# One core, three fused transformer blocks: branch products of the third block from rounded parts, and held chunks in its two last token projections

## The chip, the cores and the metric

The kernel runs on one core of one Trainium2 chip, in one launch. The metric is the device time of that core in microseconds. Two engines matter most here: PE (TensorE) does the matrix products, ACT (ScalarE) and DVE (VectorE) prepare operands and take results out of PSUM. POOL and SP mostly issue DMAs.

## The reference

Three blocks follow each other on x, 512 tokens by 1024 features, in fp32. The change touches only the end of the third one. `h` and `h2` are modulated norms of x; `ret`, `four`, `sgu` are the retention, Fourier and gated branches.

```
z = h @ w_in                                   # ..., gates (3 x 1024)
ga, gb, gc = split(sigmoid(gates), 3)
merged = ga*(ret @ w_a) + gb*(four @ w_b) + gc*(sgu @ w_c)   # ret: 512 wide, four and sgu: 256 wide
y = merged @ w_o
x = x + gt1 * rms_norm(y, g_post_mix)
h2 = rms_norm(x, g_pre_mlp) * (1 + sc2) + sh2
a = relu(h2 @ w_up)
x = x + gt2 * rms_norm((a*a) @ w_down, g_post_mlp)
```

## The kernel before

**Layout.** Features lie on the 128 partitions, so a tensor of 1024 features is 8 tiles of 128x512 (features by tokens). Weights come in chunks of 512 KB (128x1024 floats) through a ring of four SBUF slots, `weight_ring` (`c.slot`), by DMAs that SP issues in the order of the list STAGES. A stage of kind "loop" or "branch" is a hardware loop on every engine.

**Split products.** Most stages compute an fp32 product from rounded parts: ACT copies a weight chunk into `weight_hi` (type fp32r, `round_chunk`), DVE writes the rest `weight - hi` into `weight_lo` (`rest_chunk`), and PE adds three products: hi with hi, hi with lo, lo with hi, each a 128x512 matmul. `weight_hi` and `weight_lo` hold two chunks (SPLIT_RING = 2), so chunk n+2 can be rounded only when the products with chunk n are done. Activations have such parts too: `H_hi`/`H_lo`, `mid_hi`/`mid_lo`. The semaphore `w_rounded` counts ACT's rounds, `w_split` DVE's rests; SP refills a slot when its chunk is split. Stages that are not split use the fp32 operands directly; PE's trace then shows two MATMUL records for each product.

**Banks.** Two rings of four PSUM banks each: `proj_banks` for the projections, `mix_banks` for everything else. PE waits for a bank's `empty` semaphore and raises `full`.

**The stages at the change**, in the order in which PE works:

- The Fourier product ("four", L1470 and L1471) and the 32 small products of the gated branch ("sgu", L1478) end the mixing. DVE turns the two sgu banks into `cond` tiles (L2285); ACT copies the four banks out.
- "br", the branch stage (L1480 to L1507 on PE, `gate_tiles` on ACT, `branch_tiles` on DVE): eight output tiles, each from four chunks. Three chunks hold the gates' weights and make three split products of 24 matmuls (L1498). The fourth holds the columns of w_a, w_b and w_c for this tile; it is not split: PE multiplies it directly with `T(8..11)` and four `late_tile`s (L1505), 4 + 2 + 2 fp32 products into three banks. PE waits for the mixed branches (`mixed`, `four`, `sgu_ready`) ahead of the whole loop. ACT takes the gates out with a sigmoid, DVE multiplies and adds, and splits the merged tile into two parts (`merged_hi`, `merged_lo`).
- "ro", the output projection, a token stage (`token_stage`, L1509 to L1546): output tiles are 128 tokens by 512 features, two halves (`part`) of four token tiles each, every half contracted over four chunks. The chunk is the outer loop, the four token tiles the inner one, except that the last two chunks of the second half are contracted by token tile: all of token tile 0 first, then tile 1, and so on, so that tiles end one after another. These two chunks (6 and 7) are "held": their parts go to a place of their own (`c.held`) instead of the ring of two. `root_token`, `root_residual` on ACT and `gained`, `new_residual`, `token_scales` on DVE turn each token tile into the new x and its norm's scale.
- The hand-over to "upr" (the MLP's up projection) goes by halves of 256 tokens: `half_turned` (L1554) turns x back to features by tokens and scales it, into four banks "ht"; ACT (`round_half`) writes the rounded part, DVE (`split_half`) recomputes the unrounded value from the same bank and subtracts; `half_pair` multiplies the first two tiles of upr, first with the rounded part (L1568), then with the rest (L1572). Then follows the loop `split_loop` (L875).
- "dnr", the down projection, is a token stage over 16 chunks a half, with its last two chunks contracted by token tile as well, but none held: chunk 31 takes the place of chunk 29 in the ring of two.

Each engine executes its instructions strictly in the order of its program; the order across engines is set by the semaphores alone. `st.done` and `st.last` make an engine also wait for its own instruction.

Of the kernel before, what the change touches and what calls it, by code (L numbers as in the profile page):

```python
# [324 lines left out]
class Chip:  # L325


    def __init__(self, nc, ctx, dram):
# [37 lines left out]
        with ExitStack() as mlstm:  # L366
# [26 lines left out]
            "pr_ready", "sgu_ready", "merged", "relu_ready", "mlp_raw", "mlp_hi", "mlp_mid", "grow_diag", "y_sq", "y_root", "x_new", "h10_root", "h10_diag", "h10_hi", "h10_raw", "h10_lo", "out_ready", "out_stored",  # L393
# [136 lines left out]
    def held(self, n):  # L530

        return tuple(self.relu_r[:, at * S:(at + 2) * S] for at in (4 * n, 4 * n + 2))
# [124 lines left out]
def sync_program(nc, sp, c):  # L657
# [14 lines left out]
    for stage in STAGES:  # L672
# [20 lines left out]
        if looped:  # L693
            per = len(pieces(kt))
            use0 = proj.number[(name, 0)]
            with sp.Fori(1, total // RING) as i:
                for q in range(RING):
                    if kind == "branch":
                        if q < 3:
                            sp.wait_ge(s["w_split"], 3 * (i - 1) + (c.first_split[name] + q + 1))  # L700
                        else:
                            sp.wait_ge(proj.full_sem, 6 * (i - 1) + (use0 + 6))
                    elif name in SPLIT:
# [13 lines left out]
def chunk_use(c, chunk):  # L717

    name = [s[0] for s in STAGES if c.first_chunk[s[0]] <= chunk][-1]
    if name in SPLIT and (name != "br" or (chunk - c.first_chunk[name]) % 4 < 3):  # L720
        n = chunk - c.first_chunk[name]
        return c.sem["w_split"], c.first_split[name] + (n if name != "br" else 3 * (n // 4) + n % 4) + 1
# [5 lines left out]
    elif kind == "branch":  # L728
        t = 6 * (n // 4) + (n % 4 if n % 4 < 3 else 5)
# [71 lines left out]
def tensor_program(nc, pe, c):  # L801
# [681 lines left out]
    use0, chunk0 = proj.number[("br", 0)], c.first_chunk["br"]  # L1483
    pe.wait_ge(s["mixed"], MIXED_M + 4)
    pe.wait_ge(*mix.emptied(("four", 1)))
    pe.wait_ge(s["sgu_ready"], 2)
    with pe.Fori(0, 4) as i:
        for j in range(12):
            u, n, g = use0 + j, j // 6, j % 6
            pe.wait_ge(proj.empty_sem[u % RING], i * 3 + u // RING)  # L1490
            ch = chunk0 + 4 * n + min(g, 3)
            if g < 3:
                sn = c.first_split["br"] + 3 * n + g
                pe.wait_ge(s["w_split"], i * 6 + (sn + 1))
                for k in range(KD):
                    w = slice(k * P, (k + 1) * P)
                    for m, (stationary, moving) in enumerate(((c.hi, hi9), (c.hi, c.H_lo), (c.lo, hi9))):
                        last = mm(proj.banks[:, u % RING, :], stationary(sn)[:, w], moving(k), start=k + m == 0, stop=k == KD - 1 and m == 2)  # L1498
                last.then_inc(proj.full_sem, 1)
                continue  # L1500
            pe.wait_ge(c.landed[ch % RING], i * 32 + 16 * (ch // RING + 1))
            srcs = [[T(8 + k) for k in range(4)], [c.late_tile(2), c.late_tile(3)], [c.late_tile(4), c.late_tile(5)]][g - 3]
            at = (0, 4, 6)[g - 3]
            for k, src in enumerate(srcs):
# [4 lines left out]
    def token_stage(name, hi, lo, held, ready=None):  # L1509
# [3 lines left out]
        def products(n, part, q, t, whole=None):  # L1513
# [3 lines left out]
            w_hi, w_lo = whole or (c.hi(first + n), c.lo(first + n))  # L1517
# [8 lines left out]
        for part in range(2):  # L1526
            for q in range(chunks if part == 0 else chunks - 2):
# [9 lines left out]
        for t in range(NB):  # L1537
            for q in range(chunks - 2, chunks):
# [1810 lines left out]
```

## Time and profile before

| what | value |
|---|---|
| median of 3 runs | 3490.22 us (3490.09 to 3494.72) |
| the profiled execution | 3490.96 us, its span 3489.3 us |
| PE busy, share of the span | 3370.3 us, 97% |
| DVE, ACT busy | 1995.6 us (57%), 1098.5 us (31%) |
| HBM traffic | 357.66 MB read, 103 GB/s over the span |

The span runs from the first to the last recorded instruction; 1.66 us of the execution lie around it. PE's matmuls are pipelined: the record of a 128x512 matmul of rounded parts lasts 389 ns, but the next one starts sooner. Intervals from start to start tell what a matmul costs, not the records' lengths. PEclk is the granted clock of TensorE, 1.00 for the upper of its two levels (2.4 GHz) and 0.50 for the lower (1.2 GHz).

### The profile page before, as it was taken

What the parts mean: (1) busy time and instruction counts of PE and PEld (TensorE: products, weight loads), DVE (VectorE), ACT (ScalarE), POOL (GpSimd) and SP (SyncE); (2) the same over time, 40 slices, a digit from 0 to 9 for tenths busy, and PEclk for the clock granted to TensorE, in tenths of its full rate; (3) what the DMA queues carried; (4) which work ended last, traced back from release to release, by engine and by line L of the source; (5) the groups of instructions that cost most, each with busy time, mean ns of one, the idle gap of its engine ahead of it and who ended that gap; (6) DMA issues with size and microseconds to landing.
All of it is one profiled execution on the core that took longest, in us unless ns stands there. A gap on an engine that the chain in (4) does not pass through costs nothing. (4 is left out here: it accounts for less than half of the span.)

```text
span 3489.3 us, 38628 instructions
## 1 busy us (share of the span) xinstructions
PE 3370.3 (97%) x13776; PEld 2507.8 (72%) x13776; DVE 1995.6 (57%) x2807; ACT 1098.5 (31%) x1491; POOL 134.1 (4%) x230
## 2 busy tenths in 40 slices
PE   6999999999899999999999999999999999999999
PEld 3446778887678887667788854678887656778887
DVE  6685666535668864465665369666634543355522
ACT  2223422224532222453333200443333341142222
POOL 1000000000000000000000040000000100000000
PEclk9999999999999999999999999999999999999999
DMA  7222355542125542212223311122333222222232
GB/s 285 79 67 85 117 187 192 172 133 66 49 97 192 192 143 86 79 43 85 85 97 96 95 55 49 54 90 96 94 99 127 67 73 79 90 85 86 94 101 81
DMA packets 100426, 361.20 MB, mean 104 GB/s; under 512 B 11152, under 2 KB 11168, under 8 KB 100064
## 3 DMA queue, kind: packets, MB, share of 16 engines
q1 hardware_dynamic: 79088, 280.34, 24.1%
q0 software_dynamic: 20080, 75.27, 6.4%
q10 hardware_dynamic: 1152, 4.19, 0.3%
q8 instruction: 65, 1.06, 0.1%
q14 instruction: 41, 0.34, 0.0%
HBM read 357.66 MB, written 2.10 MB: 103 GB/s over the span
## 5 line engine op out<-in xcount | busy, mean ns | idle before, releaser
L2285 DVE TENSOR_TENSOR weight_lo<-weight_ring,weight_hi 128x1024 fp32r<-128x1024 f32 (+1 forms) x458 | 552.9, 1208 | 941.0 <-ACT weight_hi L1599 935.4
L1599 ACT ACTIVATE weight_hi<-weight_ring 128x1024 fp32r<-128x1024 f32 (+1 forms) x458 | 478.5, 1045 | 1641.2 <-PE proj_banks L875 1001.8
L875 PE MATMUL proj_banks<-h_lo,weight_hi 128*128 128x512 f32 x1704 | 664.9, 390 | 0.0
L875 PE MATMUL proj_banks<-h_hi,weight_hi 128*128 128x512 f32 x1344 | 523.9, 390 | 4.0 <-DVE weight_lo L2285 4.0
L875 PE MATMUL proj_banks<-h_hi,weight_lo 128*128 128x512 f32 x1344 | 523.5, 389 | 0.0
L875 PEld LDWEIGHTS proj_banks<-h_lo,weight_hi 128*128 128x128 f32 x1704 | 321.0, 188 | 66.6
L875 PEld LDWEIGHTS proj_banks<-h_hi,weight_hi 128*128 128x128 f32 x1344 | 252.6, 188 | 57.9 <-issue 5.7
L875 PEld LDWEIGHTS proj_banks<-h_hi,weight_lo 128*128 128x128 f32 x1344 | 252.7, 188 | 52.7
L875 PE MATMUL proj_banks<-mid_hi,weight_hi 128*128 128x512 f32 x704 | 273.9, 389 | 0.0
L875 PE MATMUL proj_banks<-mid_lo,weight_hi 128*128 128x512 f32 x704 | 273.9, 389 | 0.0
L875 PE MATMUL proj_banks<-mid_hi,weight_lo 128*128 128x512 f32 x704 | 273.9, 389 | 0.0
L821 PE MATMUL proj_banks<-h_tiles,weight_ring 128*128 128x512 f32 x528 | 233.3, 599 | 3.5 <-ACT h_tiles L1599 3.5
L821 PEld LDWEIGHTS proj_banks<-h_tiles,weight_ring 128*128 128x128 f32 x528 | 101.8, 193 | 131.7 <-issue 129.9
L2293 DVE SCALAR_TENSOR_TENSOR scratch<-proj_banks,vectors,scratch 128x511 f32<-128x511 f32 (+3 forms) x208 | 155.2, 746 | 26.3 <-ACT scratch L1599 12.7
L2285 DVE TENSOR_TENSOR scratch<-scratch 128x512 f32<-128x512 f32 (+6 forms) x218 | 154.3, 708 | 12.2 <-ACT scratch L1599 2.5
L875 PEld LDWEIGHTS proj_banks<-mid_lo,weight_hi 128*128 128x128 f32 x704 | 132.2, 188 | 27.5
L875 PEld LDWEIGHTS proj_banks<-mid_hi,weight_hi 128*128 128x128 f32 x704 | 132.2, 188 | 27.4
L875 PEld LDWEIGHTS proj_banks<-mid_hi,weight_lo 128*128 128x128 f32 x704 | 132.2, 188 | 27.4
L2293 DVE SCALAR_TENSOR_TENSOR scratch<-scratch,vectors 128x512 f32<-128x512 f32 x190 | 142.9, 752 | 6.7
L1599 ACT ACTIVATE scratch<-proj_banks 128x512 f32<-128x512 f32 (+1 forms) x178 | 100.7, 572 | 117.5 <-PE proj_banks L821 68.2
L1599 ACT ACTIVATE scratch<-proj_banks,vectors 128x512 f32<-128x512 f32 x112 | 83.9, 749 | 159.9 <-PE proj_banks L821 159.9
L1599 ACT ACT_TABLE_LOAD x70 | 89.8, 1283 | 54.6 <-PE proj_banks L821 13.3
(402 smaller groups left out, 5132.3 us busy)
## 6 DMA issues: line engine op xcount, KB each, us to landing
weight_ring<-in_w_up SPq DMA_DIRECT2D x176, 512.0 KB, 3.3
ada_ring<-in_ada POOLq DMA_DIRECT2D x96, 512.0 KB, 3.8
weight_ring<-in_w_dn SPq DMA_DIRECT2D x64, 512.0 KB, 3.5
weight_ring<-in_w_br SPq DMA_DIRECT2D x32, 512.0 KB, 3.2
weight_ring<-in_w_upr SPq DMA_DIRECT2D x32, 512.0 KB, 3.2
weight_ring<-in_w_dnr SPq DMA_DIRECT2D x32, 512.0 KB, 3.2
weight_ring<-in_w_dn SPq DMA_DIRECT2D x32, 384.0 KB, 3.1
cond<-in_ada POOLq DMA_DIRECT2D x20, 512.0 KB, 4.6
```

Source lines behind the costliest of these rows:

```text
L821: last = mm(bank[:, 0:n], c.slot(chunk)[:, i * P:(i + 1) * P], rhs(k), start=k == 0, stop=k == sum(per) - 1)
L875: last = mm(proj.banks[:, u % RING, :], stationary(split0 + n)[:, w], moving(k), start=k + m == 0, stop=k == kt - 1 and m == 2)
L1599: return nc.scalar.activation(out, in_, func, **kw)
L2285: return v.tensor_tensor(out, a, b, op)
L2293: return v.scalar_tensor_tensor(out=out, in0=a, scalar=x, in1=b, op0=op0, op1=op1)
```

## The change

- The fourth chunk of each branch tile is split too (`splits_of`: 32 rounds instead of 24), and the branch products become three products of rounded parts. The eight branch operands get rounded parts: ACT's `branch_round` writes them to `H_hi`, DVE writes the rests to free tiles. PE's three waits ahead of the loop go; it waits for `branch_lo`, k by k, inside the branch products.
- ro: chunks 5, 6 and 7 are held, and these three are contracted by token tile.
- The residual's square sum is one ACT instruction over 1024 values instead of two over 512 with an addition of eps between them.
- The hand-over: PE turns half 1 ahead of the products with half 0's rests; the unrounded values of two of the four ht banks (1 and 3) are made by ACT (`raw_half`) instead of DVE; the order of the rests is 0, 1, 4, 5, 2, 3, 6, 7; several self-waits go; the scales of token tiles 2 and 3 are made inside DVE's `split_half(0)`.
- dnr: chunk 31 is held in `h_rounded`; the squares that used this place as scratch go elsewhere.

```diff
 def splits_of(stage):
-    return 24 if stage[0] == "br" else chunks_of(stage)
+    return chunks_of(stage)
...
+    def branch_hi(self, k):
+        return self.H_hi(k)
+
+    def branch_lo(self, k):
+        if k < 4:
+            return self.mid_hi[:, (8 + k) * S:(9 + k) * S]
+        return self.late_r[:, (k - 2 if k < 6 else k) * S:(k - 1 if k < 6 else k + 1) * S]
+
+    def held(self, name, n):
+        if name == "ro" and n >= 5:
+            return tuple(self.relu_r[:, at * S:(at + 2) * S] for at in (4 * (n - 5), 4 * (n - 5) + 2))
+        if name == "dnr" and n == F3T - 1:
+            return tuple(self.h_r[:, at * S:(at + 2) * S] for at in (4, 6))
+        return None
...
# PE, branch stage
-    pe.wait_ge(s["mixed"], MIXED_M + 4)
-    pe.wait_ge(*mix.emptied(("four", 1)))
-    pe.wait_ge(s["sgu_ready"], 2)
     with pe.Fori(0, 4) as i:
         for j in range(12):
             u, n, g = use0 + j, j // 6, j % 6
             pe.wait_ge(proj.empty_sem[u % RING], i * 3 + u // RING)
-            ch = chunk0 + 4 * n + min(g, 3)
-            if g < 3:
-                sn = c.first_split["br"] + 3 * n + g
...
-            pe.wait_ge(c.landed[ch % RING], i * 32 + 16 * (ch // RING + 1))
...
-                last = mm(proj.banks[:, u % RING, :], c.slot(ch)[:, (at + k) * P:(at + k + 1) * P], src,
-                          start=k == 0, stop=k == len(srcs) - 1)
+            sn = c.first_split["br"] + 4 * n + min(g, 3)
+            pe.wait_ge(s["w_split"], i * 8 + (sn + 1))
+            at, count = ((0, KD), (0, KD), (0, KD), (0, 4), (4, 2), (6, 2))[g]
+            hi, lo = (hi9, c.H_lo) if g < 3 else (c.branch_hi, c.branch_lo)
+            for k in range(at, at + count):
+                if g >= 3:
+                    pe.wait_ge(s["branch_lo"], k + 1)
+                w = slice(k * P, (k + 1) * P)
+                for m, (stationary, moving) in enumerate(((c.hi, hi), (c.hi, lo), (c.lo, hi))):
+                    last = mm(proj.banks[:, u % RING, :], stationary(sn)[:, w], moving(k), start=k == at and m == 0,
+                              stop=k == at + count - 1 and m == 2)
             last.then_inc(proj.full_sem, 1)
...
# PE, token stages
-            for q in range(chunks - 2, chunks):
-                last = products(chunks + q, 1, q, t, held and held(q - chunks + 2))
+            for q in range(chunks - together, chunks):
+                last = products(chunks + q, 1, q, t)
...
-    for half in range(2):
-        half_turned(half)
-        half_pair(half)
+    half_turned(0)
+    half_pair(0)
+    half_turned(1)
+    half_rest(0)
+    half_pair(1)
+    half_rest(1)
...
+REST_ORDER = (0, 1, 4, 5, 2, 3, 6, 7)
...
# ACT
+    for h in range(4):
+        branch_round(h, T(8 + h))
     for t in range(2):
+        act.wait_ge(*mix.filled(("four", t)))
+        branch_round(4 + t, mix.bank(("four", t)))
         copy_out(mix, ("four", t), c.late_tile(2 + t))
+    for t in range(2):
+        act.wait_ge(s["sgu_ready"], t + 1)
+        branch_round(6 + t, c.late_tile(4 + t))
...
-            for g in range(3):
-                u = u0 + 6 * n + g
+            for g in range(4):
+                u = u0 + 6 * n + (g if g < 3 else 5)
                 act.wait_ge(proj.full_sem, i * 12 + u + 1)
-                ahead = 3 * n + g + SPLIT_RING
+                ahead = 4 * n + g + SPLIT_RING
...
     def root_residual(t):
-        for p in range(2):
-            act.wait_ge(s["x_new"], 2 * t + p + 1)
-            st.link(f(T(32).rearrange("p (k f) -> p k f", k=4), c.x_token(t, p), ACT.Square, accum_out=c.x_stat(p, t)))
-            if p == 0:
-                st.link(f(c.x_bias(t), c.x_stat(0, t), ACT.Identity, scale=1.0 / D, bias=eps))
-        st.done(f(c.x_scale(t), c.x_stat(1, t), ACT.Sqrt, scale=1.0 / D, bias=c.x_bias(t)), s["h10_root"])
+        act.wait_ge(s["x_new"], 2 * t + 2)
+        x = c.x[:, :].rearrange("p (k j f) -> p k j f", k=KD, j=NB)[:, :, t, :]
+        st.link(f(c.T(55, 2).rearrange("p (k f) -> p k f", k=KD), x, ACT.Square, accum_out=c.x_stat(0, t)))
+        st.done(f(c.x_scale(t), c.x_stat(0, t), ACT.Sqrt, scale=1.0 / D, bias=eps), s["h10_root"])
...
+    def raw_half(half):
+        use, layer, part, _ = MODULATED[10]
+        for b in (1, 3):
+            for k in range(2 * b, 2 * b + 2):
+                if half == 1:
+                    act.wait_ge(s["h10_lo"], KD)
+                bank = mix.bank(("ht", half, b))[:, k % 2 * 256:(k % 2 + 1) * 256]
+                ins = f(c.raw_half(k), bank, ACT.Identity, scale=c.g(use, k), bias=c.m(layer, part, k))
...
-    round_chunk("ro", 5)
-    for n in range(2):
-        round_to("ro", 6 + n, c.held(n)[0])
+    for n in range(5, KD):
+        round_to("ro", n, c.held("ro", n)[0])
...
     round_half(0)
-    for t in range(2, 4):
-        root_residual(t)
+    root_residual(2)
+    root_residual(3)
+    raw_half(0)
     for n in range(SPLIT_RING):
         round_chunk("upr", SPLIT_RING + n)
     round_half(1)
+    raw_half(1)
...
-    for n in range(17, F3T):
+    for n in range(17, F3T - 1):
         round_chunk("dnr", n)
+    round_to("dnr", F3T - 1, c.held("dnr", F3T - 1)[0])
...
# DVE
+    for k in range(KD):
+        dve.wait_ge(s["branch_hi"], k + 1)
+        if k in (4, 5):
+            dve.wait_ge(*mix.emptied(("four", k - 4)))
+        tt(c.branch_lo(k), c.branch_raw(k), c.branch_hi(k).bitcast(F32), ALU.subtract).then_inc(s["branch_lo"], 1)
...
             for g in range(3):
...
+                rest_br(i, 4 * n + g + SPLIT_RING, last)
             for g in range(3):
                 u = u0 + 6 * n + 3 + g
...
+            rest_br(i, 4 * n + 3 + SPLIT_RING, last)
...
     def split_half(half):
-        for b in range(4):
-            dve.wait_ge(s["h10_hi"], KD * half + 2 * b + 2)
+        for b in (0, 2, 1, 3):
+            bank = mix.bank(("ht", half, b))
+            if half == 0 and b == 1:
+                for t in range(2, 4):
+                    token_scales(t)
+            if b % 2 == 0:
+                dve.wait_ge(s["h10_hi"], KD * half + 2 * b + 2)
...
+            else:
+                dve.wait_ge(*mix.emptied(("ht", half, b)))
```

## Rows read from the trace of the kernel before

**Rows 1.** The page: busy time of each engine, share of the span, instructions.

```profile
PE 3370.3 (97%) x13776; PEld 2507.8 (72%) x13776; DVE 1995.6 (57%) x2807; ACT 1098.5 (31%) x1491; POOL 134.1 (4%) x230
```

**Rows 2.** Waits of PE from 2870 us on: us in total, times, longest.

```profile
PE proj_banks L1498 <- DVE cond L2285: 4.0, 1, 4.0
PE proj_banks L1572 <- DVE h_lo L2285: 2.7, 3, 1.2
PE proj_banks L1523 <- DVE weight_lo L2285: 2.4, 1, 2.4
PE mix_banks L1554 <- DVE scratch L2289: 2.2, 2, 1.7
```

**Rows 3.** Stretches: us, busy time of PE, PEld, DVE, ACT, POOL, granted clock, DMA, GB/s.

```profile
2882.40:2887.60 5.20, 5.18 (x12) 4.14 (x13) 0.00 (x0) 0.00 (x0) 0.00 (x0) 0.51 0.00 0
2887.60:3070.10 182.50, 182.50 (x693) 130.01 (x692) 63.15 (x76) 38.53 (x50) 0.00 (x0) 1.00 0.24 84
...
3140.00:3143.50 3.50, 3.50 (x11) 2.76 (x10) 2.51 (x5) 1.08 (x2) 0.00 (x0) 0.51 0.00 0
3471.00:3474.40 3.40, 3.40 (x10) 2.67 (x9) 0.00 (x0) 0.00 (x0) 0.00 (x0) 0.52 0.00 0
```

**Rows 4.** Timeline, mixing to branch stage: start us, us, instruction [idle before].

```profile
2876.42 1.97 PE L1478 MATMUL mix_banks<-cond,scratch 128*64 128x128 f32 x32
...
2876.59 0.60 ACT L1599 ACTIVATE ada_ring<-mix_banks 128x512 f32<-128x512 f32 x1 [1.10 <-PE mix_banks L1471]
...
2877.20 1.28 ACT L1599 ACT_TABLE_LOAD   x1
...
2881.28 0.69 DVE L2285 TENSOR_TENSOR cond<-cond,scratch 128x512 f32<-128x512 f32 x1
...
2882.42 0.79 PE L1498 MATMUL proj_banks<-mid_hi,weight_hi 128*128 128x512 f32 x1 [4.03 <-DVE cond L2285]
```

**Rows 5.** The chain that ended last, one branch tile: start us, us, what.

```profile
2908.27 16.33 PE proj_banks L1498 x72
2924.61 6.87 PE proj_banks L1505 x16
```

**Rows 6.** Timeline, branch stage: a round, its rest, an evacuation.

```profile
2901.52 1.06 ACT L1599 ACTIVATE weight_hi<-weight_ring 128x1024 fp32r<-128x1024 f32 x1 [3.97 <-PE proj_banks L1498]
...
2902.61 1.22 DVE L2285 TENSOR_TENSOR weight_lo<-weight_ring,weight_hi 128x1024 fp32r<-128x1024 f32 x1 [4.29 <-ACT weight_hi L1599]
...
2908.31 0.69 DVE L2285 TENSOR_TENSOR scratch<-proj_banks,scratch 128x512 f32<-128x512 f32 x1 [0.30 <-PE proj_banks L1505]
```

**Rows 7.** Timeline, output projection, second half: statistics, then rests of held chunks.

```profile
3093.26 0.30 ACT L1599 ACTIVATE small<-small,others 128x4 f32<-128x4 f32 x1
...
3095.90 2.35 DVE L2285 TENSOR_TENSOR relu_hi<-weight_ring,relu_hi 128x1024 fp32r<-128x1024 f32 x2
```

**Rows 8.** Timeline, token tile 0 after its last product.

```profile
3106.08 0.60 ACT L1599 ACTIVATE scratch<-proj_banks 128x512 f32<-128x512 f32 x1 [5.70 <-PE proj_banks L1523]
...
3107.72 1.54 DVE L2293 SCALAR_TENSOR_TENSOR x_tiles<-scratch,small,x_tiles 128x512 f32<-128x512 f32 x2
```

**Rows 9.** Timeline, hand-over to the up projection.

```profile
3115.90 3.84 PE L1554 MATMUL mix_banks<-scratch,x_tiles 128*128 128x128 f32 x32 [1.70 <-DVE scratch L2289]
...
3117.18 4.75 ACT L1599 ACTIVATE late_rounded<-mix_banks,mod,gain 128x256 fp32r<-128x256 f32 x8 [0.88 <-PE mix_banks L1554]
...
3118.58 1.12 DVE L2290 TENSOR_SCALAR scratch<-mix_banks,gain,mod 128x256 f32<-128x256 f32 x2
...
3119.50 4.08 PE L1568 MATMUL proj_banks<-late_rounded,relu_lo 128*128 128x256 f32 x32
...
3135.95 2.02 PE L1572 MATMUL proj_banks<-h_lo,relu_lo 128*128 128x256 f32 x12
...
3140.01 0.57 PE L875 MATMUL proj_banks<-late_rounded,weight_hi 128*128 128x512 f32 x1
```

**Rows 10.** Timeline, down projection: first product of its two last chunks.

```profile
3470.62 0.50 PE L1523 MATMUL proj_banks<-weight_hi,h_rounded 128*128 128x512 f32 x1 [2.41 <-DVE weight_lo L2285]
```

More of the change, by code:

```diff
@@ L528, in ro_out, with branch_raw, raw_half @@
         return self.T(24 + 4 * p + t)
-    def held(self, n):
-        return tuple(self.relu_r[:, at * S:(at + 2) * S] for at in (4 * n, 4 * n + 2))
+    def branch_raw(self, k):
+        return self.T(8 + k) if k < 4 else self.late_tile(k - 2)
+    def branch_hi(self, k):
[10 more added lines that the diff above has]
+        return None
+    def raw_half(self, k):
+        return self.pool[:, 12 * S + k * 256:12 * S + (k + 1) * 256]
     def first_up(self, t):
@@ L697, in sync_program @@
                 for q in range(RING):
[L698 to L703, printed above, removed]
+                    if name in SPLIT:
                         sp.wait_ge(s["w_split"], RING * (i - 1) + (c.first_split[name] + q + 1))
@@ L719, in chunk_use @@
     name = [s[0] for s in STAGES if c.first_chunk[s[0]] <= chunk][-1]
[L720 to L722 removed]
+    if name in SPLIT:
+        return c.sem["w_split"], c.first_split[name] + chunk - c.first_chunk[name] + 1
     _, kind, tiles, kt = STAGE[name]
@@ L1507, in tensor_program, with token_stage, products @@
             last.then_inc(proj.full_sem, 1)
-    def token_stage(name, hi, lo, held, ready=None):
+    def token_stage(name, hi, lo, together, ready=None):
         chunks, first = STAGE[name][3] // 2, c.first_split[name]
-        def products(n, part, q, t, whole=None):
+        def products(n, part, q, t):
             key = (name, NB * part + t)
             bank = open_bank(proj, key) if q == 0 else proj.bank(key)
-            w_hi, w_lo = whole or (c.hi(first + n), c.lo(first + n))
+            w_hi, w_lo = c.held(name, n) or (c.hi(first + n), c.lo(first + n))
@@ L1526, in token_stage @@
         for part in range(2):
-            for q in range(chunks if part == 0 else chunks - 2):
+            for q in range(chunks if part == 0 else chunks - together):
                 n = chunks * part + q
@@ L3082, in vector_program, with rest_br @@
         st.done(tt(c.late_tile(4 + t), c.late_tile(4 + t), T(35 + t), ALU.mult), s["sgu_ready"])
-    u0 = proj.number[("br", 0)]
+    for k in range(KD):
[3 more added lines that the diff above has]
+        tt(c.branch_lo(k), c.branch_raw(k), c.branch_hi(k).bitcast(F32), ALU.subtract).then_inc(s["branch_lo"], 1)
+    u0 = proj.number[("br", 0)]
+    def rest_br(i, ahead, last):
+        if last and ahead >= 8:
+            rest_chunk("ro", ahead - 8)
+            return
+        split, chunk = c.first_split["br"] + ahead, c.first_chunk["br"] + ahead
+        dve.wait_ge(s["w_rounded"], i * 8 + (split + 1))
+        tt(c.lo(split), c.slot(chunk), c.hi(split).bitcast(F32), ALU.subtract).then_inc(s["w_split"], 1)
     def branch_tiles(i, last=False):
@@ L3089, in branch_tiles @@
             for g in range(3):
-                ahead = 3 * n + g + SPLIT_RING
-                if last and ahead >= 6:
-                    rest_chunk("ro", ahead - 6)
-                else:
-                    split, chunk = c.first_split["br"] + ahead, c.first_chunk["br"] + 4 * (ahead // 3) + ahead % 3
-                    dve.wait_ge(s["w_rounded"], i * 6 + (split + 1))
-                    tt(c.lo(split), c.slot(chunk), c.hi(split).bitcast(F32), ALU.subtract).then_inc(s["w_split"], 1)
+                rest_br(i, 4 * n + g + SPLIT_RING, last)
             for g in range(3):
@@ L3163, in vector_program @@
         gained("ro", 0, t, c.ro_out(t, 0), c.gain_row(0, 0), 0)
-    rest_chunk("ro", 5)
-    for n in range(2):
-        rest_to("ro", 6 + n, c.held(n))
+    for n in range(5, KD):
+        rest_to("ro", n, c.held("ro", n))
     for n in range(2):
@@ L3175, in vector_program @@
     split_half(0)
-    for t in range(2, 4):
-        token_scales(t)
     for n in range(SPLIT_RING):
@@ L3216, in vector_program @@
         gained("dnr", 0, t, c.late_tile(t), c.gain_row(1, 0), 8)
-    for n in range(17, F3T):
+    for n in range(17, F3T - 1):
         rest_chunk("dnr", n)
+    rest_to("dnr", F3T - 1, c.held("dnr", F3T - 1))
     for t in range(NB):
```

87 lines of the change are left out of this document (42 added, 45 removed).

## Prediction, made before the changed kernel had been run

> **What bounds the kernel now.** The page first: PE is busy for 97% of the span, DVE for 57%, ACT for 31% [rows 1]. So the time is PE's, and an edit can bring only three things: less work for PE, fewer waits of PE, or less time at the lower clock. The waits of PE in the last 620 us are few: 4.0 us ahead of the branch stage, 2.2 and 2.7 us in the hand-over to upr, 2.4 us near the end of dnr [rows 2]. The stretches show the clock: it is 1.00 in 2887.6 to 3070.1, but 0.51 to 0.52 in three short stretches that begin at or just behind such a wait, 5.2, 3.5 and 3.4 us long [rows 3]. The chain gives the price of a branch tile: 72 products of the gates in 16.33 us, which is 0.2268 us each, then 8 direct fp32 products (16 records) in 6.87 us, 0.859 us each [rows 5].
>
> **The start of the branch stage.** PE's last small products end at 2876.42 + 1.97 = 2878.4; it then waits for DVE's second `cond` tile, ready at 2881.97, and starts at 2882.42 [rows 4]. The gates need none of it, and after the change nothing holds them: 4.0 us less. The 5.2 us at 0.51 behind it [rows 3] cost 5.2 x 0.49 = 2.5 us, of which I leave 0.4 for a first product that is slow in any case (0.79 us [rows 4]). Together 6.1 us. If the small products, not the wait, bring the clock down, only 4.0.
>
> What is added lies beside the gates. ACT: six rounds and two copies while the mixing ends, the last two rounds behind DVE's `cond` tiles, 0.60 us each [rows 4]: done at about 2882.7; then its table load and a tiny instruction, 1.5 us: 2884.2. Gate 0's products end at 2878.4 + 5.44 = 2883.8, so the round of chunk 2 (1.06 us [rows 6]) ends at 2885.3. DVE: eight rests at about 0.72 us with the gap (0.69 [rows 4]) from 2882.0 on, to 2887.8, and behind them in its queue the rest of chunk 2 (1.22 us [rows 6]), 2889.0. PE wants chunk 2 after two gates, at 2889.3. It fits, by 0.3 us; I take 0 and keep up to 1 us for it. The new waits for `branch_lo` come at 2894.7: long satisfied.
>
> **The branch products.** Eight fp32 products (6.87 us) become 24 of rounded parts: 24 x 0.2268 = 5.44 us. 1.43 us x 8 tiles = **11.4 us** [rows 5]. This stands if the rounding keeps up. Each tile adds one round and one rest, so ACT has 4 x 1.06 + 3 x 0.58 = 6.0 us of work and DVE 4 x 1.22 + 6.3 = 11.2 us (three multiplications and two additions at 0.69, the merged tile's split at about 1.1, gaps) in 21.8 us. Before they had 38.5 and 63.2 us in 182.5 [rows 3]. The order holds too: the branch chunk is rounded when gate 1 is done and split 2.6 us later, 2.8 us before product a wants it; the next tile's second chunk is rounded when product c is done, split behind two evacuations some 2.7 us later, and wanted 5.44 us later. Queued behind it on DVE are the two instructions for the merged tile, which ro wants only chunks later. SP refills a slot at the split instead of after the products: earlier, never later; the bytes stay the same. Cost of all this: 0, its cover the 21.8 us of PE. The waits inside the products, 64 in all, I price at 0: the gates' loop has two satisfied waits for each 24 products and still runs at 0.2268 us a product [rows 5]. The upper bound is the first product after a change of operands, recorded with 0.79 us where an ordinary one has 0.39, so 0.4 us each [rows 4].
>
> **ro with three held chunks.** PE was done with ro at 3115.90 - 1.70 = 3114.2 [rows 9]. Four token tiles of 12 products (10.9 us) and two whole chunks (10.9 us) lie ahead of that, so the second half began at 3092.4. Now chunk 4 is done at 3097.85, and all rests must be there: ACT's statistics end at 3093.56 [rows 7], three rounds follow, and DVE's third rest ends at 3095.90 + 2.35 = 3098.25 [rows 7]; these instructions and their order stay, only their targets change. PE waits 0.5 us. Then four token tiles of 18 products, 4.08 us each, from 3098.4 to 3114.7: 0.5 us later than before. In exchange the tiles end further apart. From a tile's end to its new x are 3.2 us (3106.08 to 3107.72 + 1.54 [rows 8]). Tile 2 ends at 3110.6, its x is there at 3113.9, and behind it in DVE's queue the scales of tile 1 at 3114.4, for ACT has only one square of about 1.06 us to do (as a round of 1024 values [rows 6]) and a root. So half 0 is turned at 3114.8 rather than 3115.90: **1.1 us**. The wait of 1.7 us is gone, half a us of it comes back as the wait for rests.
>
> **The hand-over.** Before: 3115.90 to 3140.01, 24.1 us [rows 9]. Now: the turn takes 3.6 us (3115.90 to 3119.50), to 3118.4; the 32 products with rounded parts 3.9, to 3122.3. The next turn needs the scales of tile 3. Its x is there at 3118.0; ACT is busy with the rounds of half 0 until about 3120.4 (eight took 4.75 us [rows 9]), then two squares with their roots, 1.5 us each, to 3123.4, then DVE's 0.5: 3123.9. So PE's next wait is here, 1.5 us. Turn to 3127.5; half 0's 16 rests, 2.0 us, which have been ready since about 3127 (12 took 2.02 at worst [rows 9]), to 3129.5; rounded parts of half 1 to 3133.4, for ACT's `raw_half(0)` and two weight rounds (4 us) leave its rounds of half 1 at 3127.5 to 3132; the rests, whose last needs ACT's raw values at 3134 and DVE's 0.9, to 3135.4. That is 20.6 us, **3.5 us** less: DVE's 1.12 us for a pair of raw values [rows 9] no longer stand four times in each half's path.
>
> The clock fell to 0.51 at 3140.0 [rows 3] after a series of short waits; 3.5 x 0.49 = 1.7 us. Waits of 0.5, 1.5 and some 0.3 us remain, so I leave this fall in. The Trainium skill (TensorE: Matmul & The Clock Gate, section on psum-queue depth-cycling) says that frequent micro-idles between groups of matmuls let the clock swing between its levels. By this rule too the fall stays, and my sum is unchanged; without it the sum would be 1.7 us better. The trace agrees, with no wait over 1.7 us in this stretch and a clock of 0.51 behind it.
>
> **dnr.** The wait of 2.4 us at 3470.62 is for chunk 31's round and rest, which follow chunk 29 [rows 2, 10]. Held, chunk 31 follows chunk 30's round at once, a chunk earlier. The wait goes, and the fall behind it, 3.4 x 0.48 = 1.6 us [rows 3]: **4.0 us**. The tail behind PE stays.
>
> **Sum.** 6.1 + 11.4 + 1.1 + 3.5 + 4.0 = 26.1 us off the profiled execution's 3490.96 us: 3464.9. The median lies 0.7 us lower: **3464.1 us**. With the lower bounds (3.0, 11.0, 0.4, 1.5, 2.6) it is 18.5 us, 3471.7; with the upper ones (6.4, 11.6, 1.6, 6.0, 4.4) 30 us, 3460.2.
>
> **Rivals.**
> - *The clock takes back.* It falls at the branch stage all the same (2.1 us) and a second time in the hand-over (1.7 us, as at 3140). For it: the products at 2876.42 use half the array's columns, and all waits in the hand-over stay short. Against: those rows show one fall in the hand-over, not two. Median 3490.2 - 22.3 = 3467.9.
> - *The hand-over gains more.* ACT without self-waits is quicker than 0.59 us a round, the third wait shrinks and the clock holds: 3.5 + 1.7 + 1 more, 3461.
> - *The new waits cost.* 64 x 0.4 = 25.6 us: nothing is left, 3489.7. Against: the gates' rate.
> - *Slower: the branch chunk comes late.* Place: PE's wait for `w_split` ahead of product a. If it is over 4.8 us late against my schedule (2.8 us of slack, then 2 us), PE waits 2 us in each tile, and each wait brings a fall of some 2.5 us as at 2882.4: 8 x 4.5 = 36 us, 3500. It decides from a loss of 3.3 us a tile, and costs over 0.2% from 4.1. Against: both preparing engines are over 40% idle in this stage.
> - *The change does not do what it says* at dnr or at the first wait: another semaphore of the same moment, a DMA's, holds PE. Then 4 to 6 us of the gain are missing, 3469.
>
> **Chances.** Forecast 0.70, clock 0.12, more gain 0.07, missing wait 0.06, waits that cost 0.03, slower 0.02. Differences under about 0.2% (7 us) a measurement of this kernel can't tell from none. Hence faster 0.95, same 0.03, slower 0.02. The range takes in both clock cases and most of the missing wait: 3459.5 to 3471.
>
> **What would show it.** Right: no wait ahead of L1498 and a granted clock of 1.00 from its start; a branch tile in 21.8 us instead of 23.2; the turn of half 0 at the end of ro with no wait, a wait of 1 to 2 us ahead of the turn of half 1; no PE wait in dnr. Wrong: a wait for `weight_lo` inside the branch stage, products there over 0.23 us apart, or a hand-over over 23 us.

## The result, and the profile after

| | before | after |
|---|---|---|
| median | 3490.68 us (4 runs, 3490.09 to 3494.72) | 3464.94 us (4 runs, 3461.79 to 3468.48) |
| profiled execution | 3490.96 us, span 3489.3 | 3468.48 us, span 3466.8 |

The ratio is 0.9924, with a 95% interval of 0.9907 to 0.9941. The forecast was 3464.1 us, in a range of 3459.5 to 3471.

The page of the kernel after, to be read beside [rows 1]:

```profile
PE 3355.3 (97%) x13840; PEld 2517.3 (73%) x13840; DVE 2003.4 (58%) x2815; ACT 1110.9 (32%) x1503; POOL 134.1 (4%) x230
```

PE has 64 records more (192 for the branch products instead of 128) and is busy for 15 us less: three products of rounded parts take less than a direct one, and behind 2880 us less time passes at the lower clock (ahead of it more, see `after_again`).

PE's waits from 2850 us on, in the columns of [rows 2]:

```profile
PE mix_banks L1560 <- DVE scratch L2331: 0.9, 1, 0.9
PE proj_banks L1529 <- DVE relu_hi L2327: 0.4, 1, 0.4
PE mix_banks L1479 <- ACT ada_ring L1613: 0.4, 1, 0.4
```

The waits of 4.0 us ahead of the branch stage and of 2.4 us in the down projection are gone, and those of the hand-over have shrunk from 4.9 to 0.9 us. One of 0.4 us is new, on a rest of the three held chunks. (The last row is ahead of the change, where the kernel before has the same wait.)

How the late stages lie, in the columns of [rows 3]: branch stage, output projection, hand-over, up projection, down projection.

```profile
2884.90:3059.10 174.20, 174.20 (x770) 144.29 (x769) 79.45 (x97) 47.25 (x59) 0.00 (x0) 1.00 0.28 94
3059.10:3103.30 44.20, 43.77 (x193) 35.78 (x191) 24.14 (x34) 19.59 (x35) 0.00 (x0) 1.00 0.32 107
3103.30:3123.20 19.90, 19.00 (x161) 18.75 (x161) 15.24 (x34) 17.14 (x35) 0.00 (x0) 1.00 0.17 54
3123.20:3286.40 163.20, 163.20 (x722) 135.19 (x722) 85.69 (x116) 45.88 (x60) 0.00 (x0) 1.00 0.28 93
3286.40:3460.40 174.00, 174.00 (x770) 144.07 (x768) 51.41 (x55) 39.26 (x50) 0.00 (x0) 1.00 0.26 88
```

The granted clock is 1.00 in all five. The kernel before had 0.51 to 0.52 in three stretches of this part [rows 3].

From stage start to stage start, read off the first product of each stage in both traces:

| stretch | before | after | gain | forecast |
|---|---|---|---|---|
| first gated product to the first gate product | 6.0 | 1.9 | 4.1 | 4.0 |
| branch stage | 187.7 | 174.2 | 13.5 | 2.1 + 11.4 |
| output projection to the first turn | 45.8 | 44.3 | 1.5 | 1.1 |
| hand-over | 24.1 | 19.9 | 4.2 | 3.5 |
| up projection | 164.8 | 163.2 | 1.6 | 0 |
| down projection to the start of its last product | 178.2 | 173.9 | 4.3 | 4.0 |
| tail | 6.3 | 6.5 | -0.2 | 0 |
| sum, from unrounded values | 612.9 | 583.8 | 29.1 | 26.1 |

But the first gated product, the last piece ahead of the change, starts at 2882.99 us here and at 2876.42 before [rows 4], 6.6 us later, in code that both kernels share. So the profiled execution gained 22.5 us, the changed part 29.1. The run `after_again` deals with this.

The start of the branch stage, PE's timeline of the kernel after:

```profile
2882.99 1.97 PE L1492 MATMUL mix_banks<-cond,scratch 128*64 128x128 f32 x32
2884.89 0.50 PE L1511 MATMUL proj_banks<-mid_hi,weight_hi 128*128 128x512 f32 x1
```

The gates follow the small products with no idle time, at full rate. The first gate product takes 0.50 us where the one before took 0.79 [rows 4].

The chain of the kernel after, whose rows merge what [rows 5] shows apart:

```profile
2884.96 174.30 PE proj_banks L1511 x768
3059.27 21.77 PE proj_banks L1529 x96
```

The eight branch tiles are 768 products in 174.3 us without a break: 0.227 us each, 21.79 us a tile. The output projection's first half follows at the same rate.

### The profile page after: what moved, and what is told of

It reads as the page before. It is cut to its first block and busy times, and to the rows that moved or that the text cites. A ratio compares the mean times of both kernels' runs of the same rounds, so it can differ in the third digit from the quotient of the medians.

```text
span 3466.8 us, 38774 instructions
## 1 busy us (share of the span) xinstructions
PE 3355.3 (97%) x13840; PEld 2517.3 (73%) x13840; DVE 2003.4 (58%) x2815; ACT 1110.9 (32%) x1503; POOL 134.1 (4%) x230
## 3 DMA queue, kind: packets, MB, share of 16 engines
q8 instruction: 65, 1.06, 0.1%
## 5 line engine op out<-in xcount | busy, mean ns | idle before, releaser
L2327 DVE TENSOR_TENSOR weight_lo<-weight_ring,weight_hi 128x1024 fp32r<-128x1024 f32 (+1 forms) x464 | 560.2, 1208 | 914.3 <-ACT weight_hi L1613 908.0
```

The lines of the kernel that those rows point to most:

```text
L2327: return v.tensor_tensor(out, a, b, op)
```

## The experiments

All stretches below are measured in the profiled execution of each run, from the start of a stage's first product, since the time ahead of 2876 us differs between executions by more than most of the effects. The medians, beside 3490.58 us of the kernel before, are 3468.82 for `dnr_ring`, 3470.32 for `handover_back` and 3462.44 for `ro_two`; the stretches tell what these can't. `order_back`, `raw_back`, `more_waits`, `rests_late2` and `rests_late3` ran once each.

### The wait alone

`start_alone` is the kernel before with one edit.

```diff
-    pe.wait_ge(s["mixed"], MIXED_M + 4)
-    pe.wait_ge(*mix.emptied(("four", 1)))
-    pe.wait_ge(s["sgu_ready"], 2)
     with pe.Fori(0, 4) as i:
...
+            if j == 3:
+                pe.wait_ge(s["mixed"], MIXED_M + 4)
+                pe.wait_ge(*mix.emptied(("four", 1)))
+                pe.wait_ge(s["sgu_ready"], 2)
             pe.wait_ge(c.landed[ch % RING], i * 32 + 16 * (ch // RING + 1))
```

> The kernel before, with one edit: PE's three waits for the mixed branches stand ahead of the first direct branch product instead of ahead of the whole branch loop. Theory (the wait and the fall of the clock behind it are separate from the products' price): PE starts the gates 4.0 us earlier, the granted clock stays 1.00, the stretch from the first gated product (2876.4 us before) to the end of the span shrinks from 612.9 us by 6.1 us to about 606.8, a branch tile still takes 23.2 us. Rival (the small products with half the array's columns bring the clock down): only 4.0 us less, a stretch at 0.51 behind the start. Rival (the direct products take the wait over): 0 us.

Median 3483.76 us against 3490.58, ratio 0.9977 (0.9967 to 0.9988). In its trace the gates begin 1.9 us behind the first gated product, and the branch stage takes 185.3 us. Three stretches: branch stage, one inside the hand-over, up projection.

```profile
2878.30:3063.60 185.30, 185.30 (x706) 132.33 (x705) 66.64 (x82) 38.90 (x52) 0.00 (x0) 1.00 0.23 82
...
3122.90:3126.30 3.40, 3.40 (x18) 3.40 (x18) 3.06 (x6) 2.25 (x4) 0.00 (x0) 0.50 0.52 167
3133.60:3296.80 163.20, 163.20 (x723) 135.11 (x721) 85.69 (x116) 45.90 (x60) 0.00 (x0) 1.00 0.27 93
```

The clock is 1.00 in the branch stage. The gain there is 4.1 + (187.7 - 185.3) = 6.5 us, near the expected 6.1, and the small products do not bring the clock down. With the same upper clock and no wait, 185.3 against 174.2 us is the price of the products alone: **11.1 us**, with the 2.4 us of the fall apart. The whole part behind the first gated product took 603.2 us, 9.7 less than before. The other 3.2 us came from two falls of the clock: the one that stood behind the hand-over now lies inside it (second row), where it costs nothing: the hand-over still takes 24.2 us, since PE waits there for ACT and DVE anyway. And the down projection lost none:

```profile
PE proj_banks L1524 <- DVE weight_lo L2286: 2.4, 1, 2.4
```

The whole down projection of this run, in the columns of [rows 3]:

```profile
3296.80:3473.20 176.40, 174.00 (x768) 143.77 (x767) 51.39 (x55) 39.37 (x50) 0.00 (x0) 1.00 0.25 87
```

The same wait of 2.4 us as in [rows 2], but no stretch at the lower clock behind it.

### The held last chunk

`dnr_ring` is the kernel after, with chunk 31 back in the ring of two.

```diff
-    for n in range(17, F3T - 1):
+    for n in range(17, F3T):
         round_chunk("dnr", n)
-    round_to("dnr", F3T - 1, c.held("dnr", F3T - 1)[0])
```

> The changed kernel, with chunk 31 of the down projection back in the ring of two. Theory: PE waits 2.4 us for its rest again and the clock falls to half for some 3.4 us behind it; from the first product of the up projection's loop to the end 4.0 us more than in the changed kernel. Rival (the held chunk is only a by-product, the wait is a DMA's): 0 us. Rival (the clock would have stayed up): 2.4 us.

Its waits of PE in the down projection, and the stretch behind the wait:

```profile
PE proj_banks L1527 <- DVE weight_lo L2324: 2.4, 1, 2.4
```

```profile
3447.10:3450.50 3.40, 3.40 (x10) 2.63 (x9) 0.00 (x0) 0.66 (x2) 0.00 (x0) 0.50 0.00 0
```

The down projection takes 178.2 us against 173.9, 4.3 us more. In `start_alone`, with the same wait and no fall, it took 176.6, so 2.7 of them are the wait with the restart behind it and 1.6 the lower clock. The rival by which a DMA holds PE falls. The term of 4.0 us stands when a fall follows the wait, as here and in the kernel before; where none follows, the held chunk would be worth 2.7.

### The hand-over, whole and by its edits

`handover_back` is the kernel after with the hand-over's functions of before (three held chunks stay). `order_back` and `raw_back` undo one edit each.

```diff
# order_back
     half_pair(0)
-    half_turned(1)
     half_rest(0)
+    half_turned(1)
# raw_back
     root_residual(3)
-    raw_half(0)
...
     round_half(1)
-    raw_half(1)
...
-            if b % 2 == 0:
+            if True:
                 dve.wait_ge(s["h10_hi"], KD * half + 2 * b + 2)
```

> The changed kernel, with the hand-over to the up projection as before: halves one after the other, all unrounded values by DVE, two squares for a residual, self-waits back. Three held chunks stay. Theory: from the first turn to the up projection's loop 24.1 us instead of 20.0, with waits of DVE's rests and of scales, and the clock falls to 0.51 behind it: 4.1 + 1.7 = 5.8 us more in all. Rival (the fall at 3140 us before was an accident of its moment): 4.1 us. Rival (the gain comes from the earlier ends of token tiles 0 to 2, not from the hand-over's own edits): under 1 us.

> The changed kernel, with one edit of the hand-over undone: PE multiplies half 0's rests ahead of the turn of half 1. Theory: the rests of banks 1 and 3 come behind the scales in DVE's queue, so PE waits for them some 3 us after the first products, then turns half 1 and waits for the first rounded tile: 2 to 4 us more in the hand-over (19.9 us). Rival: the order is worth nothing, since the same products wait for the same rests: 0 to 0.5 us more.

> The changed kernel, with one edit of the hand-over undone: DVE makes all unrounded values, ACT none. Theory: DVE does 4 x 0.5 us more in each half, ACT 2.1 us less; in half 0 the rests still end while PE turns half 1 (0 to 1 us), in half 1 ACT's rounds start 2 us earlier but DVE's last rest ends about 1 us later: 0 to 1.5 us more in the hand-over (19.9 us). Rival: this split is what the hand-over's gain comes from: 3 to 4 us more.

`handover_back`, PE's waits for rests in the hand-over, and the stretch at the lower clock inside it:

```profile
PE proj_banks L1578 <- DVE h_lo L2305: 3.6, 3, 1.2
```

```profile
3109.00:3112.40 3.40, 2.91 (x13) 2.62 (x14) 3.10 (x5) 0.30 (x1) 0.00 (x0) 0.50 0.08 11
```

The hand-over takes 26.0 us, 6.1 more than after, near the expected 5.8 in size. But the fall lay inside the hand-over and not behind it (the up projection takes 163.2 us, its full rate). The old hand-over took 24.1 and 24.2 us in the kernel before and in `start_alone`, without a fall that cost anything. Where the other 1.9 us lie shows in PE's two turns, first of `handover_back`, then the second one of the kernel before:

```profile
3096.47 3.84 PE L1560 MATMUL mix_banks<-scratch,x_tiles 128*128 128x128 f32 x32
...
3109.99 4.98 PE L1560 MATMUL mix_banks<-scratch,x_tiles 128*128 128x128 f32 x32 [0.49 <-DVE scratch L2309]
```

```profile
3128.44 3.84 PE L1554 MATMUL mix_banks<-scratch,x_tiles 128*128 128x128 f32 x32 [0.54 <-DVE scratch L2289]
```

From the first turn to the second are 13.5 us against 12.5 before (3115.90 to 3128.44, [rows 9]), and from there to the up projection 12.5 against 11.6. The second difference, 0.9 us, is the clock: the fall lies on the turn, 4.98 us instead of 3.84. The first, 1.0 us, is not. PE turns half 0 earlier, but DVE, still at token tile 3, starts half 0's unrounded values 3.5 us behind the turn (at 3100.01), where before it started 2.7 us behind it [rows 9]; that is 0.9 of the 1.0 us. So without the fall the old hand-over would take 25.1 us behind three held chunks, and its edits are worth 5.2 us there: without them, 1.0 us of what the output projection gained is lost again. The rival by which the earlier token tiles bring the gain falls.

The two single edits, PE's waits of `order_back` and of `raw_back`:

```profile
PE proj_banks L1582 <- DVE h_lo L2327: 0.9, 1, 0.9
```

```profile
PE mix_banks L1560 <- DVE scratch L2329: 0.9, 1, 0.9
PE proj_banks L1582 <- DVE h_lo L2325: 0.9, 1, 0.9
```

`order_back`: 20.6 us, 0.6 more. Half 0's rests wait 0.9 us for DVE, but this wait stands where the other one stood: with the rests first, the scales for the second turn are ready in time. So the order is worth 0.6, nearer to its rival than to my 2 to 4. I had both waits in my account, though PE can serve one while the other runs out. `raw_back`: 21.5 us, 1.6 more, with a second wait of 0.9 us at half 1's last rests, a little above the expected 0 to 1.5. What is left, 5.2 - 0.6 - 1.6 = 3.0 us, belongs to the single square, the self-waits, the place of the scales and what the edits do only together; these were not tried apart.

The kernel after, PE and then ACT in the hand-over, beside [rows 9]:

```profile
3103.35 3.84 PE L1560 MATMUL mix_banks<-scratch,x_tiles 128*128 128x128 f32 x32
3106.95 4.08 PE L1574 MATMUL proj_banks<-late_rounded,relu_lo 128*128 128x256 f32 x32
3111.92 3.84 PE L1560 MATMUL mix_banks<-scratch,x_tiles 128*128 128x128 f32 x32 [0.90 <-DVE scratch L2331]
3115.52 2.16 PE L1582 MATMUL proj_banks<-h_lo,relu_lo 128*128 128x256 f32 x16
3117.52 4.00 PE L1574 MATMUL proj_banks<-late_rounded,relu_lo 128*128 128x256 f32 x32
3121.36 2.08 PE L1582 MATMUL proj_banks<-h_lo,relu_lo 128*128 128x256 f32 x16
```

```profile
3104.65 3.76 ACT L1613 ACTIVATE late_rounded<-mix_banks,mod,gain 128x256 fp32r<-128x256 f32 x8
...
3109.80 1.06 ACT L1613 ACTIVATE scratch<-x_tiles 128x1024 f32<-128x1024 f32 x1
...
3111.32 2.07 ACT L1613 ACTIVATE scratch<-mix_banks,mod,gain 128x256 f32<-128x256 f32 x4
```

Eight rounds take 3.76 us without the self-waits instead of 4.75, a residual's square 1.06. PE's only wait stands ahead of the second turn, 0.9 us where I had 1.5.

### Two held chunks or three

`ro_two` is the kernel after with the output projection as before: chunk 5 in the ring, two chunks by token tile.

```diff
-        if name == "ro" and n >= 5:
+        if name == "ro" and n >= 6:
...
-    token_stage("ro", ..., 3, lambda k: (s["merged_lo"], k + 1))
+    token_stage("ro", ..., 2, lambda k: (s["merged_lo"], k + 1))
```

> The changed kernel, with two held chunks in the output projection, contracted by token tile, as before; chunk 5 goes through the ring of two. Theory: the wait of 0.4 us for rests goes, but the scales of token tile 1 come after PE's last product, and PE waits 1.0 to 1.7 us ahead of the first turn: 0.5 to 1.3 us more from the start of the output projection to the up projection's loop. Rival (three held chunks bring nothing, for ACT's single square alone makes the scales early enough): 0.4 us less.

```profile
3095.00 3.84 PE L1560 MATMUL mix_banks<-scratch,x_tiles 128*128 128x128 f32 x32 [1.51 <-DVE scratch L2332]
```

From the output projection's start to the first turn 45.2 us against 44.3: **0.9 us** for the third held chunk. The wait of 1.5 us is back, nearly the old 1.7 [rows 9], and the one for rests is gone. So of the 1.5 us that this stage gained, 0.9 came with the third chunk, and 0.6 with the rest of the change: 0.4 of it at the stage's first product, which lasts 0.79 us behind the direct products of the kernel before and 0.39 here, and 0.2 in the shorter wait.

### Do waits on PE cost?

`more_waits` puts a satisfied wait ahead of each of the 768 products.

```diff
                 for m, (stationary, moving) in enumerate(((c.hi, hi), (c.hi, lo), (c.lo, hi))):
+                    pe.wait_ge(s["mixed"], MIXED_M)
                     last = mm(...)
```

> The changed kernel, with a wait on a long satisfied semaphore ahead of every product of the branch stage, 768 more waits. Theory (a satisfied wait on PE is hidden by the product that runs): a branch tile takes 21.8 us as before, the stage 174.2 us. Rival (each wait costs what I feared in the prediction's third rival, up to 0.4 us): 768 x 0.4 = 307 us more; at 0.02 us each 15 us more.

```profile
2876.20 174.30 PE proj_banks L1512 x768
```

174.30 us for the stage, to the hundredth what it took without them. A satisfied wait on PE costs nothing behind a running product of 0.227 us; this rival had a chance of 0.03 and deserved less.

### Where slower would begin

`rests_late2` and `rests_late3` let DVE do two or three reductions that nobody needs ahead of each rest in the branch stage; no result changes.

```diff
         dve.wait_ge(s["w_rounded"], i * 8 + (split + 1))
+        for extra in range(3):
+            at = 8 + 3 * (ahead - SPLIT_RING) + extra
+            v.tensor_reduce(small[:, at:at + 1], c.slot(chunk), AX.X, ALU.add)
         tt(c.lo(split), c.slot(chunk), c.hi(split).bitcast(F32), ALU.subtract).then_inc(s["w_split"], 1)
```

> The changed kernel, with two extra reductions of 1.22 us each on DVE ahead of every rest in the branch stage: every rest is 2.4 us late. Theory (slack of 2.8 us for three of four chunks, 2.1 us for the one behind the evacuations): the stage takes 174.2 us plus 8 x 0.3 us plus up to 1.5 us at its start, 177 to 178 us. Rival (DVE has no slack worth the name in this stage): 8 x 4 x 2.4 = 78 us more.

> The changed kernel, with three extra reductions on DVE ahead of every rest in the branch stage: every rest is 3.7 us late. Theory (the slower rival of the prediction begins where the slack of 2.1 to 2.8 us ends): each tile loses 3 x 0.8 + 1.5 = 3.9 us, the stage takes about 205 to 208 us, and with waits of 0.8 to 1.5 us the clock falls at times. Rival (the ring of two evens it out over a tile, since DVE has 21.8 us for 26 us of work at most): under 10 us more.

`rests_late2`: 186.3 us, 12.1 more than 174.2; I expected 3 to 4. DVE's timeline shows the cause (the last row is PE's):

```profile
2943.63 2.35 DVE L3142 TENSOR_REDUCE small<-weight_ring 128x1 f32<-128x1024 f32 x2 [1.96 <-ACT weight_hi L1613]
...
2945.89 1.22 DVE L2327 TENSOR_TENSOR weight_lo<-weight_ring,weight_hi 128x1024 fp32r<-128x1024 f32 x1
...
2947.90 0.69 DVE L2327 TENSOR_TENSOR scratch<-proj_banks,scratch 128x512 f32<-128x512 f32 x1 [0.19 <-DVE scratch L2327]
...
2951.15 2.35 DVE L3142 TENSOR_REDUCE small<-weight_ring 128x1 f32<-128x1024 f32 x2 [0.23 <-DVE scratch L2327]
...
2953.41 1.22 DVE L2327 TENSOR_TENSOR weight_lo<-weight_ring,weight_hi 128x1024 fp32r<-128x1024 f32 x1
...
2954.69 0.50 PE L1511 MATMUL proj_banks<-mid_hi,weight_hi 128*128 128x512 f32 x1 [1.31 <-DVE weight_lo L2327]
```

The rest for the next tile's first chunk now ends at 2947.1, and the evacuations of products a, b and c queue behind it. Products a and b are already done; against the kernel after, the evacuations end some 1.2 us later in the tile, and only then do the reductions and the rest of the next tile's second chunk begin. It ends at 2954.6, 3.5 us late where I had counted 2.4, and PE has waited 1.3 us. In the kernel after the same two rests run free of each other:

```profile
2902.64 1.23 DVE L2327 TENSOR_TENSOR weight_lo<-weight_ring,weight_hi 128x1024 fp32r<-128x1024 f32 x1 [4.21 <-ACT weight_hi L1613]
...
2908.77 1.23 DVE L2327 TENSOR_TENSOR weight_lo<-weight_ring,weight_hi 128x1024 fp32r<-128x1024 f32 x1
```

The second of them ends 3.3 us into the tile and is wanted at 5.44, so its slack is 2.1 us (the prediction had 2.7). But the slack is not 2.1 us for each chunk. The two rests (2.4 us) and the five evacuating instructions between them (some 3.6) lie in one stretch of 7.4 us, 2902.64 to 2910.00, and two late rests draw together on what DVE has left in it. I had looked at each rest by itself.

`rests_late3`: 214.6 us, 40.4 more than the kernel after; expected were 31 to 34.

```profile
PE proj_banks L1511 <- DVE weight_lo L2327: 24.6, 16, 3.3
```

```profile
2877.70:3092.20 214.50, 189.95 (x768) 150.64 (x769) 179.45 (x186) 47.22 (x59) 0.00 (x0) 0.94 0.23 76
```

PE waits in all eight tiles, 24.6 us in 16 waits, and the clock is at 0.94 on average; most of the other 15.8 us are stretches at the lower level. A tile loses 5.0 us, and the run took 3501.9 us against 3489.98 for the kernel before, slower by 0.34% (one execution of each); from the first gated product to the end it took 624.6 us against 612.9. So the slower rival exists, with waits and falls together as described. Where it begins was not measured: a loss of 1.5 us a tile in `rests_late2` is still faster, one of 5.0 slower, and the 4.1 that I had put lies between. It takes some 3.5 us more on DVE for each of the 32 rests.

### The kernel after again, and an earlier order

> The changed kernel itself, timed again beside the kernel before. From the first gated product to the end of the span its trace showed 583.8 us against 612.9 us, a gain of 29.1 us, but the medians differ by 25.7. Theory: stretches at the lower clock ahead of 2876 us, in code that both kernels share, differ from execution to execution by some 3 us each way, and the gain by the medians of more runs comes to 27 to 31 us. Rival: the changed kernel is slower by some 3 us ahead of the branch stage in every execution; then the first gated product starts at about 2883 us again and the medians differ by 24 to 27 us.

Six runs: 3457.53 to 3468.27 us, median 3467.0, ratio 0.9923 (0.9911 to 0.9936). The chain of its profiled execution:

```profile
2881.58 1.90 PE mix_banks L1492 x32
2883.48 174.30 PE proj_banks L1511 x768
```

The first gated product starts at 2881.5 us (the chain shows the next one), and from there to the end are 583.9 us, as in the first profile. In the profiles of the ten other experiments, all with the same code ahead of the change, this product starts at 2873.7 to 2876.8 us, but for 2881.9 in `order_back`, so the later start is not the changed kernel's own. A part of the difference shows in the granted clock of some early stretches, first of the kernel before, then of the kernel after:

```profile
800.00:900.00 100.00, 93.46 (x404) 71.42 (x405) 59.29 (x74) 62.12 (x86) 0.00 (x0) 1.00 0.20 68
...
1450.00:1600.00 150.00, 136.95 (x526) 96.39 (x524) 91.51 (x111) 71.45 (x89) 0.00 (x0) 0.98 0.16 53
2200.00:2300.00 100.00, 94.63 (x380) 67.75 (x379) 63.72 (x80) 51.21 (x71) 0.00 (x0) 1.00 0.20 69
```

```profile
800.00:900.00 100.00, 94.63 (x392) 72.35 (x390) 55.67 (x68) 59.11 (x84) 0.00 (x0) 0.95 0.18 61
...
1450.00:1600.00 150.00, 138.72 (x523) 97.75 (x522) 86.81 (x104) 70.38 (x88) 0.00 (x0) 0.95 0.15 50
2200.00:2300.00 100.00, 94.61 (x363) 65.64 (x362) 64.56 (x81) 48.65 (x68) 0.00 (x0) 0.98 0.19 64
```

In such stretches the clock fell more often in one execution than in the other. Added up ahead of this product, the lower level was granted for 99.0, 95.6 and 95.6 us in the three profiles that start late (`after`, `after_again`, `order_back`), and for 78.5 to 88.7 us in the ten others. At half the rate, the 10.3 us that `after` has more than the kernel before (88.7) cost up to 5.1 of the 6.6 us; the rest was not traced. The ten runs of the kernel after lie in two groups, 3457.5 to 3462.3 (four) and 3467.0 to 3468.5 (six); those of the kernel before beside them lie at 3489.6 to 3491.4, with two at 3496, one at 3495 and one at 3486. Neither theory is met in full: the falls do differ from execution to execution, but the medians differ by 23.8 us, and the kernel after has more of its runs in the upper group. With an early part of equal length it would gain 29; why its executions fall into the longer pattern more often stays open.

`earlier` tries to win the two waits that are left.

```diff
+    round_to("ro", 5, c.held("ro", 5)[0])
     for t in range(NB):
         square_token("ro", 0, t, c.ro_out(t, 0))
...
     for t in range(NB):
+        if t == 3:
+            root_residual(2)
         root_token("ro", t, c.ro_out(t, 1))
...
     round_half(0)
-    root_residual(2)
     root_residual(3)
```

(DVE takes chunk 5's rest ahead of the first half's evacuations, in the same way.)

> The changed kernel, with chunk 5 of the output projection rounded and split ahead of the first half's statistics, and the residual square of token tile 2 ahead of the root of token tile 3. Theory: the wait of 0.4 us for chunk 7's rest and most of the 0.9 us ahead of the second turn go: 0.8 to 1.2 us less between the start of the output projection and the up projection's loop. Rival: tile 3's root, now 0.8 us later on ACT, sets the second turn: 0.4 us less at most. In the medians neither is seen.

Output projection 43.5 us (0.7 less), hand-over 20.1 (0.2 more): together 0.5 us. The wait for rests is gone; the one ahead of the second turn has grown from 0.9 to 1.1 us, because tile 3's root comes later, as the rival had it. Its median, 3461.77 us (3461.15 to 3468.69, 5 runs), is no evidence of more. It is a version that is shorter in the trace by 0.5 us and can't be told from the kernel after in time.

## Why the prediction was right, point by point

The forecast was 0.8 us from the first median, but two errors cancelled in that: the changed part gained 29.1 us and not 26.1, and the early part, which I took as equal, was longer by 6.6 and 5.1 us in the two profiles of the kernel after. So the close hit of the number is partly luck; the median of all ten runs is 3467.0 us, 2.9 above the forecast and inside the range.

- **The start of the branch stage**, forecast 6.1: 6.5, by `start_alone` 4.1 of idle time and 2.4 of clock. That the small products would bring the clock down fell. The step "it fits, by 0.3 us" was too tight: the rest of chunk 2 ended 1.2 us ahead of its products, since eight rests in a row took 0.6 us each and not 0.72.
- **The branch products**, forecast 11.4: 11.1. The tile went from 23.2 to 21.8 us, as computed. The waits inside cost nothing.
- **The output projection**, forecast 1.1: 1.5. Both halves of the step showed: 0.4 us of wait for the rests (forecast 0.5) and no wait ahead of the first turn. The edit itself is worth 0.9.
- **The hand-over**, forecast 3.5: 4.2. The term was undersized where I left ACT's rounds at 0.55 us and more; without self-waits they take 0.47, and PE's wait ahead of the second turn is 0.9 us instead of 1.5. The sum credited the gain to DVE's 1.12 us for a pair of raw values; `raw_back` shows 1.6 us for that edit, and 3.0 of the 5.2 us were not told apart.
- **The clock behind the hand-over**, forecast 0, measured 1.6: the step that failed. I argued that waits of 0.5, 1.5 and 0.3 us would keep the fall at 3140 us. With 0.4 and 0.9 us left the clock stayed at 1.00 behind the hand-over, and so it did in all ten profiles that keep the new hand-over or all but one edit of it. The rule on micro-idles in the Trainium skill (TensorE: Matmul & The Clock Gate, section on psum-queue depth-cycling) is not refuted by this. The three profiles with the old hand-over, with 3.6 to 4.9 us of short waits between the last rests of the output projection and the up projection, each had a fall in or behind it, and the ten others, with 1.1 to 2.4 us, had none. I kept the fall without a measured case of so few waits.
- **The down projection**, forecast 4.0: 4.3, and `dnr_ring` shows both parts of it.
- **Rivals.** "The hand-over gains more" (chance 0.07) is what happened: 0.7 us more than forecast inside it, through ACT's quicker rounds and a shorter wait, and 1.6 us from the clock. "The clock takes back", "the new waits cost" and "the change does not do what it says" fell. "Slower" was real as a mechanism and far away.

## What to carry to other kernels

When one engine is busy for 97%, price an edit by that engine's interval from start to start, and then ask of every wait whether a stretch at the lower clock stands behind it: in this kernel a wait of 4.0 us, one of 2.4 and a series of five short ones (4.9 us in all) each had a fall behind it, and the three falls cost another 5.6 us together. Test the slack of a helper engine over the whole stretch in which its instructions queue, not instruction by instruction: rests that are late one at a time push the evacuations between them. And where executions differ by several us in code that was not changed, compare from the last common instruction on; the up projection took 163.2 us in 12 of 13 profiles, while two medians of one kernel lie 2 us apart. And ask what an earlier start does to the engine behind: the third held chunk let PE turn earlier, and with the old hand-over DVE was not ready to follow.

## What was not expected of the hardware

The same wait has its fall of the clock in one execution and none in another: PE waited 2.4 us for the down projection's last rest in the kernel before, in `dnr_ring` (0.50 to 0.52 behind it for 3.4 us) and in `start_alone` (1.00 for the whole stage). What a fall costs depends on which products it meets, also where PE often waits: the hand-over of `start_alone` had 3.4 us at 0.50 from 1.0 us behind its second turn's start and still took 24.2 us, against 24.1 without; in `handover_back` the same length met that turn's first products and cost 0.9 us. And 768 additional satisfied waits changed a stage of 174.30 us by less than 0.01 us.
